# Second layer of a two-layer hybrid trunk: where the normalised rows live, and which weights are loaded ahead of the expert stage

## What is computed

```python
def moe(h, router_w, router_b, w1, w3, w2):
    t = h.reshape(-1, D)
    aff = jax.nn.sigmoid((t @ router_w).astype(jnp.float32))
    sel = aff + router_b.astype(jnp.float32)
    ...   # best group of 4 experts, best 2 in it, their weights: gates
    a = jnp.einsum('nd,edf->nef', t, w1)
    b = jnp.einsum('nd,edf->nef', t, w3)
    hid = jax.nn.silu(a) * b * gates[..., None].astype(t.dtype)
    return jnp.einsum('nef,efd->nd', hid, w2).reshape(B, L, D)

x = x + g2x * moe(rmsnorm(x, norm2_g) * (1 + sc2x) + sh2x, router_w, router_b, moe_w1, moe_w3, moe_w2)
```

## Time and profile before

| | us |
|---|---|
| median of three runs | 1157.05 |
| the three runs | 1155.04, 1157.05, 1159.86 |
| the profiled execution's own time | 1148.31 |
| its span, first to last instruction | 1146.6 |
| mean granted TensorE clock | 0.93 |

### The profile page before, as it was taken

The page is one execution under the profiler, slowest core; times in us unless marked ns, Lnnn a source line. Parts: engine busy times, 40 slices in busy tenths (PEclk is TensorE's granted clock), DMA queues, the critical chain, the costliest instruction groups (busy, mean ns, idle before and its releaser), DMA issues.

```text
span 1146.6 us, 12445 instructions
## 1 busy us (share of the span) xinstructions
PE 974.9 (85%) x4417; PEld 537.2 (47%) x4417; DVE 451.5 (39%) x1149; ACT 272.4 (24%) x645; POOL 168.8 (15%) x204
## 2 busy tenths in 40 slices
PE   2799989979799995999999918998999698668872
PEld 0355444645476443755454404745655463433320
DVE  0305653667864245112121252266467732311103
ACT  0301213435443103021111111121436321111100
POOL 3350110201100001211212016002012000102000
PEclk8899989989999997999999968999899899889987
DMA  8962212577300009358888741522485033389973
GB/s 266 325 162 70 78 69 74 187 254 275 93 1 1 0 3 394 109 195 328 318 319 316 256 168 37 178 74 73 147 281 161 1 147 129 129 345 415 417 320 141
DMA packets 68442, 208.11 MB, mean 182 GB/s; under 512 B 10163, under 2 KB 18599, under 8 KB 59164
## 3 DMA queue, kind: packets, MB, share of 16 engines
q1 hardware_dynamic: 56416, 181.51, 42.9%
q0 software_dynamic: 9040, 16.25, 4.8%
q10 hardware_dynamic: 2924, 9.53, 2.2%
HBM read 199.99 MB, written 18.69 MB: 191 GB/s over the span
## 4 chain that ended last, share of the span: by engine, by line
PE 73%; DVE 12%; issue 5%; DMA 4%; POOL 2%; ACT 2%; ACTq 1%; SPq 0%; DVEq 0%; POOLq 0%
PE bank L1783 15%; PE bank L1701 8%; PE bank L1501 8%; PE bank L1489 8%; PE bank L1807 7%; PE bank L1411 7%; PE bank L1642 3%; PE bank L1575 3%; PE bank L1458 3%; POOL ST L1044 2%; PE bank L1553 2%; PE bank L1663 2%; PE bank L1759 2%; DMA BRANCH<-in_w_mod 1%; PE bank L1561 1%
## 5 line engine op out<-in xcount | busy, mean ns | idle before, releaser
L1783 PE MATMUL bank<-RINGW,NA 128*128 128x512 f32 (+1 forms) x448 | 176.9, 625 | 25.6 <-issue 23.2
L1783 PEld LDWEIGHTS bank<-RINGW,NA 128*128 128x128 f32 (+1 forms) x448 | 69.1, 174 | 126.4 <-issue 126.4
L1044 POOL TENSOR_TENSOR ST<-ST,RT 128x1 f32<-128x1 f32 (+4 forms) x46 | 51.4, 1117 | 502.3 <-DVE ST L1911 233.8
L1501 PE MATMUL bank<-RINGW,H 128*128 128x512 f32 (+4 forms) x384 | 119.0, 470 | 0.0
L2398 DVE SCALAR_TENSOR_TENSOR BRANCH<-BRANCH,bank 128x256 f32<-128x256 f32 x24 | 10.1, 421 | 237.9 <-ACT BRANCH L1355 237.9
L1489 PE MATMUL bank<-H,RINGW 128*96 128x512 f32 (+1 forms) x256 | 98.6, 543 | 4.0 <-ACT H L1158 2.7
L1701 PE MATMUL bank<-RINGW,H 128*128 128x512 f32 (+1 forms) x216 | 93.6, 593 | 0.0
L1501 PEld LDWEIGHTS bank<-RINGW,H 128*128 128x128 f32 x384 | 68.7, 190 | 49.4 <-issue 45.6
L1489 PEld LDWEIGHTS bank<-H,RINGW 128*96 128x96 f32 x256 | 41.6, 165 | 56.7 <-issue 51.9
L1701 PEld LDWEIGHTS bank<-RINGW,H 128*128 128x128 f32 (+1 forms) x216 | 40.6, 190 | 50.1 <-issue 50.0
L1411 PE MATMUL bank<-IDENT,WORK 128*128 128x128 f32 (+1 forms) x244 | 34.7, 291 | 34.3 <-DVE WORK L1913 33.2
(11 more groups left out here) (280 smaller groups left out, 1414.0 us busy)
## 6 DMA issues: line engine op xcount, KB each, us to landing
RINGW<-in_moe_w SPq DMA_DIRECT2D x56, 1024.0 KB, 11.3
RINGW<-in_w_mod SPq DMA_DIRECT2D x23, 2048.0 KB, 8.2
W2R<-in_moe_w SPq DMA_DIRECT2D x15, 1024.0 KB, 5.4
PROJ<-in_moe_w SPq DMA_DIRECT2D x11, 1024.0 KB, 16.8
WORK<-in_moe_w SPq DMA_DIRECT2D x8, 1024.0 KB, 18.6
RINGW<-in_w_in SPq DMA_DIRECT2D x4, 1536.0 KB, 8.3
RINGW<-in_w_out SPq DMA_DIRECT2D x4, 1536.0 KB, 10.7
RINGW<-in_w_in SPq DMA_DIRECT2D x2, 2048.0 KB, 9.4
```

Source lines behind the costliest of these rows:

```text
L1044: pool.tensor_tensor(r[:, 0:w], m[:, 0:w], POOL_HALF[:, 0:w], ALU.pow).then_inc(rstd_ready, 1)
L1501: ins = pe.matmul(bank_of(s)[:, 0:nn], HT[:, kk, t * P:(t + 1) * P], wv[:, kk, off:off + nn], start=kk == 0, stop=kk == KD - 1)
L1783: ins = pe.matmul(bank_of(s)[seats, :], XGT[n % 2][:, kk, seats], w[:, kk, :], start=kk == 0, stop=kk == KD - 1)
```

## The change

Four things, all but one in the second layer:

1. `h2_row` names where the "h2T" step puts the finished rows: in the first layer `XS` (WORK) as before, in the second `XG[0]` and `XG[1]`, the first two gather areas in the tile BRANCH. ScalarE writes them there, stores them to DRAM from there, and TensorE's "xT" of rounds 0 and 1 reads them there.
2. So WORK has its last reader in "hT". SP's wait for the first piece in WORK (expert 9) becomes a wait for the last "hT"; the wait for the stored rows and for "xT" of round 1 goes.
3. A gather into `XG[0]` or `XG[1]` must not come before "xT" of round 1 has read them: POOL waits for that from "xg" 3 on. The line has no condition on the layer, so "xg" 3 and 4 of the first layer get the wait too.
4. `w2_after` names six w2 loads ahead of the second layer's first piece (experts 0, 8, 1, 9, 2, 10) where there were four; those of 2 and 10 no longer follow the piece of expert 10.

```diff
@@ -99,8 +99,8 @@
     half = N_E // 2
     if e == 0:
-        return [0, half, 1, half + 1]
-    return [e - half, e] if e >= half + 2 else []
+        return [0, half, 1, half + 1, 2, half + 2]
+    return [e - half, e] if e >= half + 3 else []
@@ -767,6 +767,9 @@
+        def h2_row(l, t):
+            return XS[:, t, :] if l < DEPTH - 1 else XG[t - 2]
+
@@ -913,8 +916,7 @@
                 elif home[i] == SLOTS:
-                    sp.wait_ge(h2_stored, 16 * sum(len(tiles_q(m)) for m in range(DEPTH)))
-                    sp.wait_ge(*full_of(("xT", DEPTH - 1, DIRECT - 1, 1)))
+                    sp.wait_ge(*full_of(("hT", DEPTH - 1, 2, 1, 3)))
@@ -1081,8 +1083,8 @@
-                    if e >= DIRECT + 3:
-                        pool.wait_ge(*full_of(("xT", l, e - 3, 1)))
+                    if e >= 3:
+                        pool.wait_ge(*full_of(("xT", l, max(e - 3, DIRECT - 1), 1)))
@@ -1332,13 +1334,13 @@
-                    act.activation(XS[:, t, :].rearrange("p (k j) -> p j k", k=KD)[:, 64 * n:64 * n + 64, :],
+                    act.activation(h2_row(l, t).rearrange("p (k j) -> p j k", k=KD)[:, 64 * n:64 * n + 64, :],
...
-                        act.dma_start(h2_rows[t * P:(t + 1) * P, :], XS[:, t, :]).then_inc(h2_stored, 16)
+                        act.dma_start(h2_rows[t * P:(t + 1) * P, :], h2_row(l, t)).then_inc(h2_stored, 16)
@@ -1756,7 +1758,7 @@
-                                ins = pe.matmul(bank_of(s + (i,))[:, c * P:(c + 1) * P], XS[:, t, o:o + P], SEND[r][t],
+                                ins = pe.matmul(bank_of(s + (i,))[:, c * P:(c + 1) * P], h2_row(l, t)[:, o:o + P], SEND[r][t],
```

## The result

| | before | after |
|---|---|---|
| median, us | 1156.05 (4 runs) | 1142.25 (4 runs) |
| span of the runs, us | 1152.28 to 1159.86 | 1138.49 to 1147.09 |
| ratio | | 0.9873, 95% interval 0.9826 to 0.992 |
| profiled execution's span, us | 1146.6 | 1139.5 |

The change is 13.8 us faster by the medians. In a second comparison on one chip the medians were 1152.02 (11 runs) and 1140.33 (5 runs), 11.7 us, ratio 0.9894 with interval 0.9872 to 0.9916.

A forecast was written before the change was run, and what follows sets the result against it. Weight traffic was taken to bound the second layer's expert stage: 10.1 us for four pieces plus 3.75 gave 13.85, less 2.5 for the clock 11.3; 1157.05 - 11.3 = 1145.7 us, chance 0.50, range 1140.5 to 1151.

The forecast's parts named there:

- The bound: Second layer's expert stage: bound by weight traffic, share 1.00 at 407 GB/s for 103.5 us; the end follows the last first-projection pair.
- The sum to the last landing: Saturated stretch: four pieces, 10.1 us, plus 3.75 us earlier start; last landing 13.85 us earlier, 1109.83 to 1095.98.
- Feeding the rings: DMA rings after round 1: queued loads last to 1014.2, when SP issues 3 and 11; gap about zero.
- Where the weights bind again: Expert rounds: 1 to 3 run without a weight wait; loads bind from round 4, TensorE idle about 1 us before it.
- More than half of the 8.00 us comes back later as waits.: TensorE's 8.00 us wait before round 1: more than half was to return as waits in later rounds.
- The clock at the end: Last "ab", round 7: slow after a 4.8 us wait, 9.61 us instead of 7.09, losing 2.5 us.
- Alternating rounds: Rounds 4 to 7: fast, slow, fast, slow; a fast round leaves 4.8 us of waiting, a slow one 2.2.
- The gather for round 2: Before round 2's "xT": the gather lands in 9.0 to 10.4 us, stalling TensorE 0.3 to 1.5 us, taken as 1.
- rival (b): Rings run empty 1 to 5 us after a late round 2 gather; gain 6 to 10 us, 1147 to 1151, chance 0.12.
- Slower through the routing steps: Expert choice, 972 to 989: expert 9's load doubles vector operation times, losing 17 us; 3 us slower, 1160, chance 0.04.
- The rest: Rows' new address, row store, slot traffic, POOL's wait and the tail: same work or covered, POOL's new wait free.
- rival (a): Last round stays fast, its "ab" 7.09 us: gain 13.85 us, 1143.2 us, chance 0.27.

The follow-up runs named there:

- after_again: The changed kernel measured once more, unaltered, on one chip beside another variant: 1140.33 us (5 runs), ratio 0.9894 to the kernel before.
- place_only: The changed kernel with the old four early second-projection loads instead of six; ratio 0.9911 to the kernel before.
- rows_only: Changed kernel, but expert 9 still waits for round 1's "xT" and four second projections are early: 182.75 us from output projection's end (182.4 before), one run.
- warm7_short: Changed kernel plus four 128x512 matmuls with unused results ahead of the last "ab": 168.4 us from output projection's end (169.8 in the changed kernel), one run.
- warm7: Changed kernel plus eight 128x512 matmuls with unused results ahead of the last "ab"; ratio 0.9898 to the kernel before.

## Why the prediction was right, point by point

- **The bound.** Right: the saturated stretch is as dense as before and 10.8 us shorter, its end sets the last "ab". (The text ahead of the prediction calls that "ab"'s weights the last load. The second projections of 7 and 15 still land behind them, and nothing waits for those.)
- **The sum to the last landing, 13.85 us.** Right: 13.9 us in the changed kernel, and again in after_again (131.7). Its parts don't quite add up when made alone. The place gives 9.2 us (8.8 expected), the second projections 3.65 (5.05 expected), together 12.8: alone, the early second projections let the rings run dry for 1.5 us, by the share; with the place also changed round 1 ends earlier and 0.3 us are lost (rows under "Feeding the rings"). By this estimate 1.2 us come back, near the 1.1 that the parts lack.
- **Where the weights bind again.** Forecast waits were 1, 4.8, 2.2 and 4.8 us before rounds 4 to 7, measured 1.56, 5.58 (TensorE's timeline), 2.47 and 4.30. Forecast starts, taken from the end of the output projection: 81.7, 98.4, 115.1, 131.8; measured 81.0, 98.5, 115.5, 131.7.
- **"More than half of the 8.00 us comes back later as waits."** Wrong, and at odds with the forecast's own waits, which sum to 12.8 us where the four of before sum to 13.95. Measured they sum to 13.91: the 8.00 us went whole. Most of the rest of the 13.9 is that one "ab" ahead of the last was slow (round 5, 9.70 us) where three had been (rounds 1, 4 and 6, 9.62, 9.76 and 9.61 us).
- **The clock at the end.** Right in kind, wrong in size: the last "ab" is slow, but by 1.4 us and not 2.5 (8.46, and 8.56 in the second profile). That is the term of the sum that failed. I took 9.61 us from a round that had waited 5.00; after 4.27 to 4.34 us of waiting it was 8.46 to 8.79 in five places over the kernels, and 9.76 in one (round 4 before). So the gain by the profile is 12.5 us (12.7 with the tail) and not 11.3. The row of the last "ab" with its clock, 0.83:

```profile
1101.48:1109.94 8.46, 8.46 (x33) 2.85 (x34) 0.00 (x0) 0.00 (x0) 0.00 (x0) 0.83 0.29 115
```

- **Alternating rounds.** Right for the changed kernel (fast, slow, fast, slow), but not a law, as place_only shows. That it came out right owes something to luck: with 8.46 us instead of 9.70 in round 5 the waits behind would have been other ones.
- **The gather for round 2.** Wrong: I put 1 us of stall on it. The turning of round 0's hidden rows and of that gather's rows is one unbroken group at 1020.91, right behind "gbc2". The gather was issued at 1011.93 and landed in 8.6 us, at about 1020.5, where I had taken 9.0 to 10.4 us. So it was just in time:

```profile
1011.93 1.07 POOL L1088 DMA_INDIRECT BRANCH<-h_rows,IDX  x1 [11.05 <-DVE IDX L2384]
...
BRANCH<-h_rows,IDX POOLq DMA_INDIRECT x1, 8.6
```

- **Feeding the rings.** Near enough, so rival (b) falls: the rate dips to 307 GB/s in the us from 1020 and to 234 in the next, under one us of transfer by the rate and 0.3 us by the share.

```profile
1020.00:1021.00 1.00, 1.00 (x11) 1.00 (x11) 0.62 (x2) 0.74 (x2) 0.00 (x0) 1.00 0.77 307
1021.00:1022.00 1.00, 1.00 (x10) 0.76 (x8) 0.62 (x2) 0.93 (x3) 0.00 (x0) 1.00 1.06 234
1022.00:1023.00 1.00, 0.81 (x5) 0.40 (x6) 0.29 (x1) 0.60 (x1) 0.00 (x0) 1.00 0.89 377
```

- **Slower through the routing steps.** Refuted. Round 0's "ab" starts at rel 31.4 before and after, though expert 9's load now runs beside the choice of experts, and the operations of the earlier trace rows take what they took. The second of them had no traffic beside it before; now the DMA share from 990 to 992 is 1.03:

```profile
985.81 0.19 DVE L2321 TENSOR_TENSOR RT<-RT 128x32 f32<-128x32 f32 x1
...
991.78 0.19 DVE L2353 TENSOR_TENSOR BRANCH<-BRANCH 128x32 f32<-128x32 f32 x1
```

- **The rest** (rows in BRANCH, POOL's wait): nothing, by rows_only.

The measured medians differ by 13.8 and 11.7 us in the two comparisons. Both lie about the 12.5 of the profile; neither tells the forecast's 11.3 from rival (a)'s 13.85. The 1142.25 us are nearer to (a)'s 1143.2 than to the forecast's 1145.7, and only the profile shows that the last "ab" was slow and (a) did not come true. The lower end of the stated range should have been 1143.2 - 2.4 = 1140.8, not 1140.5.

## What to carry to other kernels

Where a stage is bound by weight loads, look for the last load that the end waits for and count what has to flow before it: bytes moved into an idle stretch ahead, a queue that starts earlier, and loads wanted later that can be issued behind it all count, in full only as long as the rings stay fed (the second projections alone gave 3.65 of 5.05 us). Turning further loads behind earlier rounds gave nothing: as many bytes stood ahead of the last pair. Look at what stands at the head of an in-order issue queue: one load with a late wait held up two that were free, for 3.75 us. A small tile moved to a place that is free anyway can set a large one free.

## What the runs showed of the hardware

In the twelve profiled executions of the table TensorE's "ab" of 32 matmuls took 7.03 to 7.10 us by the timeline after waits of up to 2.94 us, and 8.46 to 10.04 us after waits of 3.30 us and more, without exception. The granted clock in a slow one was a mean of 0.70 to 0.83, so part of it ran at 1.2 GHz: in round 1 of the kernel before, pairs of matmuls start 0.86 us apart at first (1015.11, 1015.99, ...) and 0.43 us apart later (1020.26, 1020.69, ...). How slow it was did not follow the length of the wait: 3.30 us were followed by 10.04, 3.32 by 8.78, 4.28 by 9.76 and 4.34 by 8.54. I had expected slow rounds of one length, and built a pattern on it.

Matmuls whose results nobody reads kept the clock at 1.00 here: 3.63 us of them made the last "ab" 1.4 us shorter (warm7_short, one run; warm7's, 7.06 us of them, also left it at 1.00).
